# Router logits summed block by block, a second scaling moved to ScalarE, and a new order of the attention steps

## What is computed

```python
for l in range(2):
    h = rms_norm(x, attn_norm_w[l])
    proj = h @ w_in[l]        # split: a_q, a_k, a_v, b_z, b_xbc, b_dt, c_q, c_k, c_v
    y_a = windowed_gqa_sink(a_q, a_k, a_v, ...)          # 6 heads
    y_b = ssd_mixer(b_z, b_xbc, b_dt, ...)               # conv, silu, softplus(dt), cumsum, 6 heads, two directions
    y_c = diff_attention(c_q, c_k, c_v, ...)             # 4 heads, two softmaxes each
    x = x + concatenate([y_a, y_b, y_c]) @ w_out[l]
    h = rms_norm(x, ffn_norm_w[l])
    # router: 4 group logits and 32 expert logits per token, group top-1, expert top-2
    g_logits, e_logits = h @ w_rg[l] + b_rg[l], h @ w_re[l] + b_re[l]
    x = x + sum over 32 experts of weight * ((silu(h @ w_gate) * (h @ w_up)) @ w_down)
return rms_norm(x, final_norm_w)
```

## Time and profile before

| | us |
|---|---|
| median of 3 runs | 1263.58 (1261.47 to 1263.85) |
| the profiled execution | 1262.58 |
| its span, first to last instruction | 1260.8 |
| TensorE matmul busy | 965.2 (77%) |
| VectorE busy | 399.0 (32%) |
| ScalarE busy | 184.9 (15%) |
| DMA queue of the weights, share of 16 engines | 434.72 MB, 83.4% |

### The profile page before, as it was taken

One profiled execution on the slowest core, in us unless ns is written; L12 is line 12 of the kernel. 1 busy time (PEld: TensorE's weight loads), 2 busy tenths in 40 slices (PEclk: granted clock), 3 DMA queues, 4 the chain that ended last, 5 costly groups with the idle time before them and its releaser, 6 DMA issues.

```text
span 1260.8 us, 26487 instructions
## 1 busy us (share of the span) xinstructions
PE 965.2 (77%) x11004; PEld 612.8 (49%) x11004; DVE 399.0 (32%) x1226; ACT 184.9 (15%) x526; POOL 8.9 (1%) x27
## 2 busy tenths in 40 slices
PE   5999989756668787886689998786666665666964
PEld 4867865433334443553377777543343333333432
DVE  2767553211112222221057574531112111111213
ACT  1245311000001110110023352110000000000001
POOL 2000000000000000000000000000000000000000
PEclk9999989888879998998899999898888888887977
DMA  9835149999999999899994242499999999999994
GB/s 343 299 127 200 46 172 411 428 424 427 426 426 423 427 423 426 341 424 428 411 400 156 82 186 92 189 427 426 426 427 425 428 426 425 427 426 424 427 425 175
DMA packets 45961, 436.62 MB, mean 346 GB/s; under 512 B 8064, under 2 KB 10112, under 8 KB 21248
## 3 DMA queue, kind: packets, MB, share of 16 engines
q1 hardware_dynamic: 45824, 434.72, 83.4%
HBM read 433.65 MB, written 1.05 MB: 345 GB/s over the span
## 4 chain that ended last, share of the span: by engine, by line
PE 42%; DMA 41%; DVE 7%; issue 5%; DVEq 2%; ACT 1%; SPq 0%; ACTq 0%
DMA ring<-in_w_up 40%; PE ps L562 16%; PE ps L638 7%; PE ps L573 4%; PE ps L761 3%; PE ps L543 2%; PE ps L582 2%; PE ps L650 2%; DMA ring<-in_w_in 2%; PE ps L701 1%; PE ps L723 1%; PE ps L708 1%; PE ps L740 1%; DVEq L1083 1%; PE ps L644 1%
## 5 line engine op out<-in xcount | busy, mean ns | idle before, releaser
L562 PE MATMUL ps<-ring,xg 128*32 128x256 f32 x4096 | 310.9, 470 | 194.5 <-DMA ring<-in_w_up 193.6
L562 PEld LDWEIGHTS ps<-ring,xg 128*32 128x32 f32 x4096 | 168.6, 134 | 321.0 <-issue 274.2
L1060 DVE SCALAR_TENSOR_TENSOR gu<-th,ps 128x128 f32<-128x128 f32 x72 | 20.8, 288 | 616.7 <-ACT th L871 616.7
L573 PE MATMUL ps<-ring,actT 128*32 128x256 f32 x2304 | 139.2, 382 | 15.3 <-issue 12.9
L573 PEld LDWEIGHTS ps<-ring,actT 128*32 128x32 f32 x2304 | 69.0, 109 | 76.4 <-DVE actT L1064 24.0
L638 PE MATMUL ps<-hT,ring 128*128 128x256 f32 x416 | 101.1, 404 | 6.3 <-DMA ring<-in_w_in 4.0
L871 ACT ACTIVATE th<-ps 128x128 f32<-128x128 f32 x72 | 19.9, 277 | 528.2 <-PE ps L562 528.2
L638 PEld LDWEIGHTS ps<-hT,ring 128*128 128x128 f32 x416 | 83.6, 204 | 20.7 <-DMA ring<-in_w_in 5.8
L582 PE MATMUL ps<-ysb,PwT 32*128 32x256 f32 x1024 | 73.3, 400 | 1.0 <-ACT ysb L875 1.0
L543 PE MATMUL ps<-xh,Pb 128*32 128x256 f32 x1024 | 69.2, 387 | 0.0
L582 PEld LDWEIGHTS ps<-ysb,PwT 32*128 32x128 f32 x1024 | 46.2, 184 | 28.9 <-issue 25.5
(11 more groups left out here) (252 smaller groups left out, 785.3 us busy)
## 6 DMA issues: line engine op xcount, KB each, us to landing
ring<-in_w_gate SPq DMA_DIRECT2D x64, 2048.0 KB, 43.0
ring<-in_w_up SPq DMA_DIRECT2D x64, 2048.0 KB, 37.4
ring<-in_w_down SPq DMA_DIRECT2D x64, 2048.0 KB, 41.9
ring<-in_w_in SPq DMA_DIRECT2D x8, 2048.0 KB, 20.0
ring<-in_w_out SPq DMA_DIRECT2D x4, 2048.0 KB, 20.3
ring<-in_w_in SPq DMA_DIRECT2D x2, 1584.0 KB, 27.3
x<-in_x SPq DMA_DIRECT2D x1, 1024.0 KB, 5.1
out<-fin SPq DMA_DIRECT2D x2, 512.0 KB, 2.7
```

The source lines that it names most:

```text
L562: last = mm(b_gate[j * SLOTS:(j + 1) * SLOTS, 0:2 * GQ], tokens[:, k, :], ring[:, low:high + 1:high - low, o:o + GQ], start=(k == 0), stop ...
L573: last = mm(b_y[j * SLOTS:(j + 1) * SLOTS, 0:DQ], actT[:, c * SLOTS:(c + 1) * SLOTS], ring[:, slot, o:o + DQ], start=(c == 0), stop=(c == ...
```

## The change

Four edits:
- `ORDER` is another list. The same steps stand in it, in another order in the attention stage, with one new step `rs2` and with `xn2` at the very end. Ahead of `y.0` stood `sc.0` to `sc.4` and `nm.0` to `nm.2`, now `sc.0` to `sc.3`, `nm.0` and `nm.1`.
- `lg` on TensorE runs over the eight blocks of the width on the outside and the two token halves on the inside, both halves summed in the same bank, and waits for each pair of blocks' copy instead of for all of them.
- `rs2` on VectorE is the reciprocal root, cut from `sq2`.
- `xn2` is ScalarE's alone: it scales both halves of xh, and stands behind `route` in its queue.

```diff
--- before.py
+++ after.py
@@ -92,21 +92,21 @@
 
 
 ORDER = """
-    sq xT.0 xT.1 xT.2 xT.3 rs xbc.0 ak par conv.0 aq.0 xbc.1 silu.0 aS.0 sc.0 xbc.2 conv.1 conv.2 silu.1 sc.1
...
-    ov
+    sq xT.0 xT.1 xT.2 xT.3 rs par conv.0 xbc.0 xbc.1 silu.0 conv.1 ak conv.2 xbc.2 xbc.3 silu.1 silu.2 conv.3
...
+    ov xn2
 """
 STEPS = [(name, *map(int, index)) for name, *index in (step.split(".") for step in ORDER.split())]
 ON_PE = {"xT", "rs", "xbc", "dt", "cq", "aq", "ak", "cum", "xs", "cb", "cumT", "rows", "aS", "cS", "y", "vz", "pT", "ck", "cv", "oa", "od",
          "yT", "cT", "outA", "outB", "fT", "lg", "seed", "rank", "ov"}
-ON_DVE = {"xc2", "hot", "sq", "xT", "par", "lam", "dt", "dta", "conv", "silu", "cum", "xdt", "seg", "row", "sc", "nm", "y", "zs", "ybn", "ycn", "sq2",
-          "xn2", "lg", "route", "rank", "ov"}
+ON_DVE = {"xc2", "hot", "sq", "xT", "par", "lam", "dt", "dta", "conv", "silu", "cum", "xdt", "seg", "row", "sc", "nm", "y", "zs", "ybn", "ycn", "sq2", "rs2",
+          "lg", "route", "rank", "ov"}
 ON_ACT = {"sq", "rs", "par", "lam", "dta", "cumT", "silu", "row", "sc", "vz", "zs", "pT", "ck", "cv", "oa", "od", "yT", "cT", "cq",
           "aq", "ak", "xs", "cb", "sq2", "xn2", "route"}
 
@@ -769,14 +769,15 @@
                             for t in range(TT):
                                 last = tr(bank[:, (a * TT + t) * P:(a * TT + t + 1) * P], xh[:, t, k * P:(k + 1) * P], ident[:, :])
                     elif kind == "lg":
-                        pe.wait_ge(done["act"], nth(li, "act", ("fT", KC // 2 - 2)))
-                        pe.wait_ge(done["dve"], nth(li, "dve", ("fT", KC // 2 - 1)))
                         pe.wait_ge(router_ready, (li + 1) * 16 * (1 + KC))
                         n = NG + NE
-                        for t in range(TT):
-                            for k in range(KC):
+                        for k in range(KC):
+                            if k % 2 == 0:
+                                by = reader(("fT", k // 2))
+                                pe.wait_ge(done[by], nth(li, by, ("fT", k // 2)))
+                            for t in range(TT):
                                 last = mm(bank[:, t * n:(t + 1) * n], hT2[:, k, t * P:(t + 1) * P], wr[:, k, :],
-                                          start=(k == 0), stop=(k == KC - 1))
+                                          start=(t == 0 and k == 0), stop=(k == KC - 1), skip_group_check=True)
                     elif kind == "seed":
 
                         for j in range(NQ):
@@ -898,10 +899,11 @@
                     elif kind == "rs":
                         last = A(xn[:, 0, 0:SEQ], bank[:, 0:SEQ], ACT.Copy)
                     elif kind == "xn2":
-                        act.wait_ge(done["dve"], nth(li, "dve", ("sq2",)))
+                        act.wait_ge(done["dve"], nth(li, "dve", ("rs2",)))
                         A(fnw[:, :], colp[:, K_FN:K_FN + KC], ACT.Copy)
                         act.wait_ge(done["pe"], nth(li, "pe", ("fT", KC // 2 - 1)))
-                        last = A(xh[:, 1, :], xh[:, 1, :], ACT.Copy, scale=st2[:, 3:4])
+                        for t in range(TT):
+                            last = A(xh[:, t, :], xh[:, t, :], ACT.Copy, scale=st2[:, TT + t:TT + t + 1])
                     elif kind == "par":
 
                         act.wait_ge(params_ready, (li + 1) * 16 * 2)
@@ -1089,13 +1091,11 @@
                         dve.wait_ge(done["act"], nth(li, "act", ("sq",)))
                         last = rsqrt(st, TT, 1.0 / D)
                     elif kind == "sq2":
-                        v.scalar_tensor_tensor(squares[:, 1, :], xh[:, 1, :], 1.0, xh[:, 1, :], ALU.mult, ALU.mult,
-                                               accum_out=st2[:, 1:2])
+                        last = v.scalar_tensor_tensor(squares[:, 1, :], xh[:, 1, :], 1.0, xh[:, 1, :], ALU.mult, ALU.mult,
+                                                      accum_out=st2[:, 1:2])
+                    elif kind == "rs2":
                         dve.wait_ge(done["act"], nth(li, "act", ("sq2",)))
                         last = rsqrt(st2, TT, 1.0 / D)
-                    elif kind == "xn2":
-                        dve.wait_ge(done["pe"], nth(li, "pe", ("fT", KC // 2 - 1)))
-                        last = v.tensor_scalar(xh[:, 0, :], xh[:, 0, :], st2[:, 2:3], None, ALU.mult)
                     elif kind == "xc2":
 
                         j = s[1]
```

More of the change, by code:

```diff
@@ L94 @@
 ORDER = """
-    sq xT.0 xT.1 xT.2 xT.3 rs xbc.0 ak par conv.0 aq.0 xbc.1 silu.0 aS.0 sc.0 xbc.2 conv.1 conv.2 silu.1 sc.1
-    xbc.3 nm.0 silu.2 aq.1 conv.3 silu.3 xbc.4 conv.4 dt aS.1 silu.4 dta xdt xs.0 xs.1 aq.2 cum aS.2 cumT nm.1
-    pT.0 cb.0 pT.1 sc.2 sc.3 seg.0.0 rows.0 seg.0.1 cb.1 nm.2 row.0.0 row.0.1 seg.1.0 seg.1.1 sc.4 vz.0 y.0 nm.3
-    row.1.0 row.1.1 seg.2.0 seg.2.1 vz.1 rows.1 row.2.0 nm.4 y.1 row.2.1 zs.0 seg.3.0 seg.3.1 row.3.0 rows.2
-    row.3.1 lam cq.0 y.2 seg.4.0 ck.0 y.3 seg.4.1 row.4.0 row.4.1 cq.1 seg.5.0 seg.5.1 row.5.0 y.4 row.5.1 zs.1
-    ck.1 pT.2 cS.0 pT.3 sc.5 sc.6 y.5 sc.7 oa.0 pT.4 cv oa.1 nm.5 ybn pT.5 yT.0 yT.1 nm.6 oa.2 sc.8 sc.9 pT.6
-    cS.1 sc.10 nm.7 outA.0 sc.11 nm.8 pT.7 outA.1 od.0 pT.8 sc.12 sc.13 outA.2 od.1 pT.9 od.2 od.3 nm.9 outA.3
-    ycn cT outB.0 outB.1 outB.2 outB.3 xc2.0 xc2.1 xc2.2 xc2.3 fT.0 fT.1 fT.2 fT.3 sq2 xn2 lg seed route rank hot
-    ov
+    sq xT.0 xT.1 xT.2 xT.3 rs par conv.0 xbc.0 xbc.1 silu.0 conv.1 ak conv.2 xbc.2 xbc.3 silu.1 silu.2 conv.3
+    xbc.4 aq.0 silu.3 xs.0 conv.4 dt aS.0 silu.4 dta aq.1 xs.1 cum cumT sc.0 aq.2 nm.0 cb.0 cb.1 sc.1 rows.0 pT.0
+    seg.0.0 seg.0.1 sc.2 nm.1 xdt row.0.0 row.0.1 aS.1 vz.0 sc.3 seg.1.0 y.0 seg.1.1 row.1.0 row.1.1 seg.2.0 lam
+    zs.0 seg.2.1 row.2.0 aS.2 nm.2 cq.0 pT.1 rows.1 y.1 row.2.1 sc.4 vz.1 seg.3.0 nm.3 seg.3.1 y.2 row.3.0
+    row.3.1 rows.2 seg.4.0 seg.4.1 row.4.0 row.4.1 ck.0 nm.4 seg.5.0 zs.1 y.3 seg.5.1 cq.1 row.5.0 y.4 row.5.1
+    ck.1 pT.2 pT.3 sc.5 cS.0 sc.6 y.5 sc.7 oa.0 pT.4 cv nm.5 oa.1 ybn pT.5 nm.6 yT.0 yT.1 oa.2 pT.6 sc.8 cS.1
+    sc.9 sc.10 nm.7 outA.0 sc.11 pT.7 sc.12 nm.8 od.0 outA.1 pT.8 sc.13 outA.2 od.1 pT.9 od.2 od.3 nm.9 outA.3
+    ycn cT outB.0 outB.1 outB.2 outB.3 xc2.0 xc2.1 xc2.2 xc2.3 fT.0 fT.1 fT.2 fT.3 sq2 rs2 lg seed route rank hot
+    ov xn2
 """
```

## The result

| | median us | lowest to highest | runs |
|---|---|---|---|
| before | 1262.87 | 1261.47 to 1263.85 | 4 |
| after | 1249.62 | 1248.57 to 1250.82 | 4 |

The ratio is 0.990, with a 95% interval of 0.9886 to 0.9915: 13.3 us less. The direction was right and half of the size was missing.

What follows compares the result with a forecast made beforehand. Expert-weight streams were taken to set the pace, so time gained before each layer's first expert hidden matmuls reaches the end. Terms -3.5, -1.7, -1.4, -0.9, +0.8 sum to -6.7 us: 1256.9, range 1252.8 to 1262.3.

Steps and rivals of the forecast that it cites:

- A: Layer 0's start: projection xbc.1, moved ahead of ak, fills TensorE's 3.97 us wait for w_in; -3.5 us, nothing in layer 1.
- B: Layer 0, 24 to 28 us: without the idle wait TensorE's clock stays at 2.4 GHz; -1.7 us, bounds 0 and -1.7.
- C: Router: VectorE's chain at L1328 starts sooner, by 1.4 us in layer 0 and 0.9 us in layer 1.
- D: Router: ScalarE scales both halves of xh behind route, hidden with 0.8 us to spare; 0.
- E: SyncE: the next layer's small parameter loads end later but 1.5 us before the next weight is due; 0.
- Rival 1: SyncE's small loads overrun and delay layer 0's first weight stream by 13 us; net +6.3, 1270 us; chance 5%.
- F: Attention stage: new TensorE wait at cum of about 1.0 us; +0.4 us a layer, bounds -0.6 and +1.6.
- G: Attention stage: score work of 3.6 us a layer moves behind y.0, covered; other steps only change place; 0, at most +3.6.

Runs made afterwards that it cites:

- e3: The kernel before with one step moved, xbc.1 ahead of ak; ratio 0.9972, -4.5 us.
- e2: The kernel before with the router edit alone, in the old order of the attention steps; ratio 0.9985, -2.3 us.
- e1: The kernel before with the new order of the attention steps and the old router; ratio 0.9921, -10.7 us.
- e5: The kernel before with one step moved, cb.1 directly behind cb.0; ratio 0.9990, -2.7 us by the medians.
- e12: The kernel before with two steps moved, xbc.1 ahead of ak and cb.1 behind cb.0; ratio 0.9984, -2.3 us.
- e6: The changed kernel with pT.0 put between cb.0 and cb.1; 1256.3 us, ratio 0.9958 to the kernel before.
- e8: The changed kernel once more, only a comment different, for a second profile; 1248.43 us in one run.
- e13: The changed kernel with aq.2 moved behind cb.0 and cb.1; 1250.9 us, ratio 0.9908 to the kernel before.
- e14: The changed kernel with aq.1 and xs.1 exchanged; 1250.9 us, ratio 0.9902 to the kernel before.
- e4: The kernel before once more, only a comment different, for a second profile; 1263.7 us in one run.
- e15: The kernel before with xs.0 moved behind aq.2; 1263.1 us, ratio 1.0001.

## Why the prediction was half right

**A, right.** -3.5 forecast; the wait went from 3.97 to 0.36 us in e3, and layer 0's "rest" fell by 2.9 us there, with the new wait of 0.56 us in it.

**B, right as a sum, wrong as a picture.** -1.7 forecast for layer 0. The two profiles of each kernel have 7.8 and 5.1 us of low time behind 23.6 us on average: half of 2.7 us is 1.35. The fall from 24 to 28 us did go, but e3, which fills the same wait, had as much low time as before: one stretch of 6.8 us at 49 us for two of half that length, at 25 and 55 us. So the idle wait was not its only cause, as the text's bounds had allowed. Over all profiles the low time is 6.8 to 20.5 us with the long wait (six) and 3.4 to 10.2 without it (twelve).

**C, right with a smaller size.** -1.4 and -0.9 forecast; L1328 stands 1.3 and 0.8 us sooner behind L770, of which 1.0 and 0.7 reach the first L562. e2, the router edit alone, gained 2.3 us.

**D, E, right.** xn2 behind route costs nothing, and the small loads ended with 1.0 us to spare (1.5 forecast). Rival 1 did not occur.

**F, right mechanism, smaller size.** +0.4 a layer forecast: a wait of 0.85 us in layer 0 of one profile, none in the other, none in layer 1, so on average 0.4 us in both layers together, for 0.8. Where it is missing, a low stretch lies on the steps ahead of it. "If that slow stretch comes back here, the wait is hidden" was the case.

**G, right on the score work.** TensorE's waits between y.0 and the last pT sum to 2.7 us in both layers, against 2.7 and 2.4 to 2.5 before. One of them is new, 0.46 us for a score step (nmx).

**The step that failed** is the end of G, "Other steps change place only; the matmuls and their shapes are the same", which put every other effect of the order at nothing, together with B, which looked for the clock's gain behind one wait of layer 0 and gave layer 1 no term at all. Layer 1 was forecast at -0.5 us and measured at -5.7. (A's "In layer 1 the weights are there and nothing is gained" held: e3's "rest" there is 146.1, as before.) Three things were outside the sum:

- cb.0 and cb.1 side by side: -1.06 us a layer, -2.1. Shown by L676 in every profile: one group where the pair is together (e1, e5, e12 and all relatives of after), two where it is apart (before, e2, e3, e6). What reaches the time is less sure: "rest" falls by 0.9 and 1.2 us in e5 and rises by 1.9 and 2.5 in e6 over the mean of after's two profiles, of which 1.08 is the other wait; but in layer 1 of e12 nothing is left of it. The listing of the two orders had shown the pair move together, and the trace of before had the 1.13 us for four; it was there to be read.
- the low clock of layer 1's attention stage: two stretches fewer, -3.4, and 0.8 less in the first hidden matmuls. Repeated in e8, e13 and e14 (absent), e4 and e15 (present). Every profile with the order and the router edit together and the pair of cb kept (eight) has two stretches there. Each edit alone (e1, e2) has three in its one profile, as has e5, so how much belongs to which is not shown, and why these stretches do not come is not settled.
- 0.6 us in layer 0's expert stage, where two profiles of one program differ by 1.6 and 2.9 us (e8, the shorter one, has the higher clock there, 0.96 against 0.94), and 0.8 us in the last stretch, which both profiles of each kernel repeat and which was not followed up.

The sum by the measured stages: layer 0 -6.6 ("rest" 136.0 to a mean of 132.1, half of the low time -1.35, router -1.0, hidden matmuls -0.35), layer 1 -5.7 (L613 to L770 -4.2, router -0.7, hidden matmuls -0.8), -0.6 and -0.8: -13.7, against 13.3 in the timed runs. That layer 0 came out near its 6.2 us is in part luck: A, B and C each brought some 0.4 to 0.6 us less than their terms (e3's 2.9, 1.35 and 1.0), and the pair of cb (1.06) and the hidden matmuls (0.35), which no term held, made up for it. Term B had treated the clock as a matter of one wait in one layer. The range followed from that: it held what a single stretch could do in layer 0, and nothing for layer 1, whose four stretches stood in the trace.

## What to carry to other kernels

Before saying that steps only change place, look at which matmuls use part of the rows: two groups on different halves that become neighbours take the time of one (1.14 for 2.26 us). Count the low-clock stretches of a stage as a term of its own, about 1.7 us each where TensorE leads, and put several of them into the range, in both signs; two profiles of one program show which belong to it. A local move in a tuned order can cost by side effects more than it saves: a bank dealt out differently (1.08 us a layer), or code that grows (10 us in a stage that the edit does not touch, about half of it low clock).
